# A third row buffer, other slots for VectorE's routing, transposes for a residual and two turnings, and a norm one slot later, in an encoder layer on one core

## The reference

```python
h = h + peer_ffn(rmsnorm(h, norm_ffn_g), peer_wq, peer_subkeys, peer_u, peer_v)

def peer_ffn(xn, w_q, sub_keys, u, v):
    q = (xf @ w_q).reshape(n, PEER_HEADS, 2, PEER_DK // 2)          # 8 heads, 2 x 128
    s = jnp.einsum('nhpd,hpkd->nhpk', q, sub_keys)                  # 128 keys a half
    sv, si = lax.top_k(s, PEER_TOPK)                                # 16 of them
    cand = sv[:, :, 0, :, None] + sv[:, :, 1, None, :]              # 256 pairs
    cidx = si[:, :, 0, :, None] * N_KEYS + si[:, :, 1, None, :]
    tv, tsel = lax.top_k(cand, PEER_TOPK)                           # 16 experts a head
    eidx = take_along_axis(cidx, tsel); g = softmax(tv)
    act = gelu(einsum('nd,ned->ne', x, u[eidx])) * g                # of 16384 experts
    return einsum('ne,ned->nd', act, v[eidx])
```

## Time and profile before

| | |
|---|---|
| median of 3 runs | 2055.32 us (2044.23, 2055.32, 2055.69) |
| profiled execution | 2047.77 us |
| its span | 2046.0 us |
| its mean granted clock | 0.988 |
| VectorE busy | 1530.7 us |
| ScalarE busy | 858.1 us |
| GpSimd busy | 718.3 us |
| HBM | 259 GB/s over the span |

### The profile page before, as it was taken

The page is one execution under the profiler, slowest core; times in us unless marked ns, Lnnn a source line. Parts: engine busy times, 40 slices in busy tenths (PEclk is TensorE's granted clock), DMA queues, the critical chain, the costliest instruction groups (busy, mean ns, idle before and its releaser), DMA issues. The chain is left out here.

```text
span 2046.0 us, 29568 instructions
## 1 busy us (share of the span) xinstructions
PE 1981.8 (97%) x11192; PEld 1765.1 (86%) x11192; DVE 1530.7 (75%) x2436; ACT 858.1 (42%) x857; POOL 718.3 (35%) x504
## 2 busy tenths in 40 slices
PE   7999998999899999999999999999999999999997
PEld 6987776998799999999999889988888888888886
DVE  5988745456678788989988987567677777778875
ACT  4340136334334554455454435433434343334343
POOL 2010110220726677587787875011001011114300
PEclk9999998999899999999999999999999999999999
DMA  5464393443344787788888787779998989998983
GB/s 207 164 193 141 116 400 137 153 168 123 127 137 156 247 275 268 272 281 286 274 272 298 265 306 283 294 274 348 340 343 328 343 326 349 364 360 345 372 314 136
DMA packets 101226, 531.27 MB, mean 260 GB/s; under 512 B 19376, under 2 KB 21568, under 8 KB 45792
## 3 DMA queue, kind: packets, MB, share of 16 engines
q1 hardware_dynamic: 71552, 408.93, 55.8%
q0 software_dynamic: 24304, 106.45, 14.4%
q10 hardware_dynamic: 5296, 14.98, 1.9%
HBM read 491.34 MB, written 38.14 MB: 259 GB/s over the span
## 5 line engine op out<-in xcount | busy, mean ns | idle before, releaser
L889 DVE TENSOR_TENSOR wl<-raw,wh 128x2048 fp32r<-128x2048 f32 x310 | 712.4, 2299 | 287.1 <-ACT wh L519 275.5
L519 ACT ACTIVATE wh<-raw 128x2048 fp32r<-128x2048 f32 x310 | 593.3, 1915 | 572.5 <-DMA raw<-in_v 408.4
L1537 PE MATMUL acc<-xhl,wh 128*128 128x448 f32 x2048 | 648.9, 377 | 12.2 <-DVE wl L889 12.2
L1538 PE MATMUL acc<-xhl,wl 128*128 128x224 f32 x2048 | 542.8, 265 | 0.0
L1537 PEld LDWEIGHTS acc<-xhl,wh 128*128 128x128 f32 x2048 | 386.7, 189 | 44.7 <-DVE wl L889 14.6
L1538 PEld LDWEIGHTS acc<-xhl,wl 128*128 128x128 f32 x2048 | 393.2, 192 | 0.0
L2025 POOL DMA_INDIRECT G<-gsum,cell x224 | 348.2, 1554 | 99.7 <-issue 74.8
L1514 PE MATMUL acc<-xhl,wh 128*128 128x288 f32 x768 | 231.7, 302 | 14.8 <-DVE wl L925 14.2
L1515 PE MATMUL acc<-xhl,wh 128*128 128x288 f32 x768 | 228.4, 297 | 0.0
L1516 PE MATMUL acc<-xhl,wl 128*128 128x288 f32 x768 | 227.9, 297 | 0.0
L1514 PEld LDWEIGHTS acc<-xhl,wh 128*128 128x128 f32 x768 | 146.5, 191 | 18.2 <-DVE wl L925 14.2
(11 more groups left out here) (306 smaller groups left out, 2638.8 us busy)
## 6 DMA issues: line engine op xcount, KB each, us to landing
raw<-in_u SPq DMA_DIRECT2D x128, 1024.0 KB
raw<-in_v SPq DMA_DIRECT2D x128, 1024.0 KB
raw<-in_w_mix SPq DMA_DIRECT2D x28, 1024.0 KB
G<-zero SPq DMA_DIRECT2D x16, 1024.0 KB, 13.8
raw<-in_w_out SPq DMA_DIRECT2D x16, 1024.0 KB
raw<-in_w_pq SPq DMA_DIRECT2D x16, 1024.0 KB
gin<-G SPq DMA_DIRECT2D x32, 512.0 KB
h<-hbg ACTq DMA_DIRECT2D x32, 448.0 KB
```

What stands on the lines that cost most here:

```text
L519: act.activation(wh[:, n % 4], raw[:, n % 4], ACT.Copy).then_inc(hi_done, 1)
L889: dve.tensor_tensor(wl[:, n % 4], raw[:, n % 4], wh[:, n % 4].bitcast(F32), ALU.subtract).then_inc(lo_done, 1)
L1537: pe.matmul(acc[:, s, 0:2 * NU], wh[:, s, j, :], xu[:, j, 0:2 * NU], start=(j == 0), stop=False)
L1538: ins = pe.matmul(acc[:, s, 0:NU], wl[:, s, j, :], xuh[:, j, :], start=False, stop=(j == DT - 1))
```

## The change

It has four parts. Routing: a third buffer `ring_a2` for own rows (the first 16 picks still use two, the other 16 use three in turn); new tables for the parts, tops, packs, sums, picks and own writes; for units of up to four heads one `wide_sum` of three operations over all 16 sums instead of 16 `gate_sum`; `own_hidden` waits for its own writes of the chunk before. Turnings: transposes instead of matmuls, behind slot 1 of iterations 29 and 30, with two banks copied out in a slot. Residual: 32 transposes ahead of V's first slot, which start the banks, the second token half first. PQ: `total(2)` behind slot 1, `scores(0, 0)` behind slot 2, and the splits for slot 3 ahead of the norm.

```diff
-XROW_IT, HST_IT = 29, 30
+XROW_IT, HST_IT, TURN_S = 29, 30, 1
+XROW_EVAC, HST_EVAC = 4 * XROW_IT + TURN_S + 1, 4 * HST_IT + TURN_S + 1
...
-PARTS = {4: (8, 1), 8: (9, 0), 12: (9, 1), 16: (4, 0), 20: (4, 1), 24: (5, 0), 28: (5, 1), 31: (10, 0), 35: (10, 1), 38: (11, 0),
-         42: (11, 1), 45: (6, 0), 49: (6, 1), 52: (7, 0), 56: (7, 1), 60: (12, 0), 64: (12, 1), 68: (13, 0), 73: (13, 1),
-         77: (14, 0), 81: (14, 1), 85: (15, 0), 90: (15, 1), 95: (16, 0), 99: (16, 1), 103: (17, 0), 107: (17, 1)}
-TOP = {12: 4, 28: 2, 42: 5, 56: 3, 73: 6, 90: 7, 107: 8}
+PARTS = {4: (8, 1), 5: (9, 0), 7: (9, 1), 12: (4, 0), 15: (4, 1), 17: (5, 0), 20: (5, 1), 29: (10, 0), 32: (10, 1), 35: (11, 0),
+         37: (11, 1), 44: (6, 0), 47: (6, 1), 49: (7, 0), 52: (7, 1), 63: (12, 0), 65: (12, 1), 68: (13, 0), 71: (13, 1),
+         79: (14, 0), 81: (14, 1), 84: (15, 0), 87: (15, 1), 101: (16, 0), 105: (16, 1), 109: (17, 0), 113: (17, 1)}
+TOP = {7: 4, 20: 2, 37: 5, 52: 3, 71: 6, 87: 7, 113: 8}
...
-SUMS = {1: 6, 2: 6, 3: 4, 5: 6, 6: 5, 7: 5, 15: 5, 17: 5, 19: 6, 31: 4, 32: 4, 33: 4, 36: 4, 37: 4, 39: 4, 40: 4, 41: 4,
-        46: 4, 47: 4, 48: 4, 51: 4, 53: 4, 54: 4, 55: 4, 57: 4, 59: 5, 61: 5, 62: 6, 63: 5, 65: 5, 66: 6,
-        76: 4, 78: 4, 79: 4, 80: 4, 82: 4, 84: 4, 86: 4, 88: 4, 93: 8, 94: 8, 96: 8, 98: 8}
+SUMS = {0: 16, 1: 16, 11: 16, 23: 8, 24: 4, 25: 8, 27: 8, 28: 4, 41: 16, 43: 16, 55: 4, 56: 8, 57: 4, 59: 8, 60: 4, 61: 4,
+        73: 8, 74: 4, 75: 8, 76: 4, 77: 8, 89: 4, 91: 8, 93: 4, 95: 8, 97: 4, 99: 4}
+WIDE_SUMS = 3
...
-           (0, 5): {4: 20}, (0, 6): {0: 21, 4: 22, 9: 23, 13: 24}, (0, 7): {0: 25, 3: 26, 8: 27, 13: 28}}
-A_CELLS = {(0, 1): 0, (1, 5): 1, (0, 3): 2, (1, 7): 3, (0, 5): 4}
...
+           (1, 7): {3: (15,), 15: (16,)}, (0, 4): {0: (17, 18)}, (0, 5): {0: (19,), 10: (20,)},
+           (0, 6): {0: (21,), 4: (22,), 9: (23,), 14: (24,)}, (0, 7): {0: (25,), 5: (26,), 11: (27,)}}
+A_CELLS = {(1, 4): 0, (0, 2): 1, (1, 6): 2, (0, 4): 3, (0, 6): 4, (0, 7): 5}
...
+def own_ring(g):
+    return g % 2 if g < K16 else (g - K16) % 3
...
 # ScalarE, pq (VectorE's the same with lo_next and norm_recip)
-                    hi_next(PQ0, i, s)
                     if first and s == 0:
+                        hi_next(PQ0, 0, 0)
+                        hi_next(PQ0, 0, 1)
                         norm_root(3, mis[:, 2], stat_done, 2)
+                    elif not (first and s == 1):
+                        hi_next(PQ0, i, s)
...
+            def wide_sum(m):
+                t, h = SUM_UNITS[m // K16]
+                u, width = HEADS * (1 - t), K16 * (h + 1)
+                eq = seq[:, 0:K16 * width].rearrange("p (r x) -> p r x", r=K16)
+                experts, gates = one(expert[:, t, 0:h + 1, :]), one(gij[:, 0, u:u + h + 1, :])
...
+                own.done(dve.tensor_tensor(eq, bcast(experts, K16, 1), bcast(expert[:, t, h, :], width, 2), ALU.is_equal))
+                own.wait(0)
+                own.done(dve.tensor_tensor(eq, eq, bcast(gates, K16, 1), ALU.mult))
+                own.wait(0)
+                dve.tensor_reduce(gsum[:, t, h, :], eq, AX.X, ALU.add).then_inc(sums_ready, K16)
...
             def act_lo(b, r):
+                if b == 1:
+                    dve.wait_ge(hst_out, 16)
...
 # TensorE, pq
-                    if first and s == 0:
+                    if first and s == 1:
                         pe.wait_ge(sq_done, 10)
                         total(2)
                         pe.wait_ge(sk_in, 16)
-                    if s > 0:
+                    if first and s == 2:
+                        scores(i, 0, first)
+                    if s > (1 if first else 0):
                         scores(i, s - 1, first)
...
-                    ins = pe.matmul(mis[:, c // 4, P * (c % 4):P * (c % 4) + P], xs4[:, c].rearrange("p q t -> p (q t)"), ident, start=True, stop=True)
+                    ins = pe.transpose(mis[:, c // 4, P * (c % 4):P * (c % 4) + P], xs4[:, c].rearrange("p q t -> p (q t)"), ident)
...
             def residual():
-                for d in range(DT):
-                    for t in range(2):
-                        ins = pe.matmul(banks[t][d // 4][:, P * (d % 4):P * (d % 4) + P], hT[:, d, P * t:P * t + P], ident, start=False, stop=False)
+                pe.wait_ge(hst_copied, 4)
+                for t in (1, 0):
+                    for d in range(DT):
+                        if t == 0 and d % 4 == 0:
+                            pe.wait_ge(acc_free, V0 + 1 + d // 4)
+                        ins = pe.matmul(banks[t][d // 4][:, P * (d % 4):P * (d % 4) + P], hT[:, d, P * t:P * t + P], ident,
+                                        start=(d % 4 == 0), stop=False, is_transpose=True)
                 ins.then_inc(res_turned, 1)
-            pe.wait_ge(hst_copied, 4)
-
-            def v_iteration(i, first=False, last=False):
+            residual()
+            def v_iteration(i, last=False):
...
                 if (t, h) in A_CELLS:
                     own_hidden(A_CELLS[t, h])
+            own_pick(28)
             own_pick(29)
-            own_hidden(5)
+            own_hidden(6)
```

## The result

The changed kernel takes 2039.22 us (median of 15 runs, 2033.26 to 2044.65) against 2052.30 (15 runs, 2044.23 to 2058.16): ratio 0.9935, 95% interval 0.9922 to 0.9947, 13 us faster. 2022 was forecast, and a saving of 29. The time lies inside the range given, by 0.8 us, only because that range was wide: 13 of the 29 us came, and the biggest term of the sum is the one that is missing. Its profiled execution took 2035.1 us with a span of 2033.3.

The account below looks back on a forecast made before the run. It took TensorE, busy 97% of the span, as the bound, plus its waits and lower-clock stretches. Savings of 5 + 13 + 6 + 5 = 29 us from a mean of 2050.8 gave 2022 us, range 2005 to 2040.

Parts of the forecast that it names:

- the rows: Product with `peer_u`: of 17.3 us lost to late splits and clock falls, 4 stay, 13 saved; pick 28 about 2 late.
- come as close: Product with `peer_u`, slots 38 and 42: picks 7 and 8 said to be as near to late as pick 28.
- Rival (1): Product with `peer_u`: rows stay late at picks 8 and 28, TensorE keeps 13 us of lateness; 2031 us, chance 0.15.
- VectorE's own work: Product with `peer_u`: with the new spread it stops TensorE nowhere; densest stretch 3 us late, under the 5 absorbed.
- The wide sums: VectorE's routing: 2.4, 3.2 and 4.0 us for units of 2, 3 and 4 heads; no change in its total.
- Three make 5.1: Product with `peer_u`: three clock falls behind waits for VectorE's split, 1.7 us each, counted in the 17.3 of lateness.
- Rival (2): The clock falls after each of three bursts of transposes, 1.7 us each; 2027 us, chance 0.08.
- The head of PQ: Start of the routing product: slot 1 ahead of `total(2)` cuts idle from 8.7 to 4.1 us; 5 saved, between 1 and 8.
- has over 5 us before slot 4: Head of PQ: ScalarE's split for slot 4 begins one slot later, with over 5 us to spare.
- Turnings: Tail of the product with `peer_u`: transposes take 1.92 us for 3.75, twice, and the idle and copy waits go; 6 saved.
- the step to V: Before the last product: 32 transposes take 3.8 us for 7.1 and hide a 1.9 wait; 5 saved, bounds 2 and 5.5.
- (5): Slower: at 2.45 us a descriptor in GpSimd's queue, TensorE stands still at slot 122; 42 lost, 2064 us, chance 0.03.

Follow-up runs that it names:

- early_picks: The changed kernel with picks 5 to 9 and 28 moved 3 to 20 writes earlier in GpSimd's queue; 2029.2 us, ratio 0.9882 to the kernel before.
- best: early_picks with ScalarE's split for PQ's slot 4 ahead of the first scores and picks 29 to 31 ahead of the last own writes; 2020.0 us, 0.9837.
- old_third: The changed kernel with the old routing tables and narrow sums, but three row buffers and picks from 21 on one place earlier; 2029.7 us, 0.9886.
- narrow: The changed kernel with the five wide sums done as 80 narrow ones in the same slots; 2036.2 us, ratio 0.9929 to the kernel before.

## Why the prediction was wrong

**The step that failed: the rows (13 us forecast, 0.3 measured).** The prediction put pick 28 in SBUF near slot 109.7 and its dot due near 109.3, a wait of 2 us with bounds at 8, and took 4 us of lateness. Its dot was due at slot 109.1, the row was there at 110.7, and VectorE waited 8.1 us. The end of unit (0,7) came at slot 107.9, close to the 107.5 forecast; what was left out are the four own writes of chunk 5, which the new `A_CELLS` puts behind that unit and so ahead of pick 28: 8.4 us. Half of the omission was hidden by luck, as the row could be read 5.6 us after its issue and not the 9.6 that the prediction took. It counted 24 own writes for the sum of the queue, but none for this place. Of the other picks, 7 and 8 were said to "come as close" and priced at nothing, and 5 and 6 weren't named; pick 7 was in time, while 5, 6 and 8 cost VectorE 2.9, 5.2 and 4.4 us, and TensorE 6.9 us ahead of slots 37 to 47. `early_picks` shows that this was all of it: with six picks moved, 3.9 us of waits and one fall of the clock (1.7 us) remained, where the prediction had taken 4 for both, and the stage was 12.5 us shorter. Rival (1), with 13 us of lateness kept and a chance of 0.15, was the mechanism, and named picks 8 and 28 for it. Its 2031 was still too low, since it kept 4 us of saving in this term and 5 in PQ.

**VectorE's own work.** That it would no longer stop TensorE was right (`best`: 3.9 us of waits). That this was needed was only half right: `old_third` gets the same time from the old spread. The wide sums cost 2.1, 2.9 and 3.7 us by the trace for 2.4, 3.2 and 4.0 forecast, and matter in nothing (`narrow`).

**The clock.** Before, three waits of 2.2 to 3.0 us had a fall behind them. After, one had (slot 37, 2.1 us), while waits of 3.0 and 2.6 us had none. "Three make 5.1" was a good account of one execution and not a price for a wait of a given length. Rival (2) was wrong: none of the four bursts of the kernel after had a fall behind it, and the falls in this stage, before and after, each stood right behind a wait of 2.1 us or more. Over the profiles of all 14 kernels here TensorE has 33 waits of 1.9 to 3.3 us in PQ and the product with `peer_u`; in 24 the clock fell before they ended or within 1.8 us behind them, in 9 it didn't.

**The head of PQ (5 forecast, 2.0 measured).** TensorE's wait was forecast as 4.1 us and was 4.2; GpSimd's sum was slowed by the second split as assumed. The step that failed is the sentence that slot 4's split "has over 5 us before slot 4": it was in time for slot 4 itself, but the copy of slot 3's queries stands behind it and the next split on VectorE. That gave 2.1 us of waiting and 1.7 of clock, against 4.5 us less of idle and 1.3 less lost to the clock behind `total(2)`: 2.0 in all. The queue behind the moved wait was followed one step too short.

**Turnings (6 forecast, 6.3 measured) and the step to V (5 forecast, 4.8 measured)** came out by their steps. The burst in the kernel after, timeline of TensorE:

```profile
1288.23 1.91 PE L1891 MATMUL mis<-cst,hT 128*32 128x128 f32 x16
```

1.9 us, without the 1.76 of idle ahead of it. The first residual's 0.6 us wait for `u_evac` lies where the prediction had put the evacuation.

**Base.** The sum was set against a mean of four executions, 2050.8; fifteen give a median of 2052.3. 1.5 us of the forecast's distance come from there. One sum in a rival is wrong too: in (5), 276 issues of 2.45 us are 676 us, 32 over the 644 and not 42, so that rival's time is 2054 and not 2064. Either lies within the 1% of no change, though the text books it as slower.

What stays open: why waits of the same length are followed by a fall of the clock once and not another time, and how far the new spread of VectorE's work helps with rows in time (1 us by the ratios of `old_third` and `early_picks`, 9 by the stage in two single profiles).

## What to carry to other kernels

When a buffer is added so that transfers can start earlier, follow each transfer's place in its issuer's queue: count every instruction between the last known point and the issue, and compare with when its reader is due, for each of them and not for one. A part that removes one wait in a chain of in-order queues is worth what the next wait leaves; the runs here went from pick 28 to pick 30 and from the sum to the query's copy. And a stage whose length wanders by several microseconds may have such a wait on its edge: with the picks moved, it was both shorter and steadier in three profiles of three.

## What the runs showed of the hardware

A long two-input operation of VectorE holds up GpSimd's indirect issues entirely, not by a share, and isn't held up by them. In the kernel after, 136 of GpSimd's indirect issues in the stage began while a split or a dot of VectorE ran; they took 2.22 us in the mean and ended 0.83 us behind the end of VectorE's instruction (half of them between 0.834 and 0.836). The 159 others took 1.0 us, also the 58 during which such an operation of VectorE began (0.97). VectorE's splits and dots took 2.29 us whether an issue was under way when they began or not. One such pair, GpSimd's the last write of (0,7), which ends 0.85 us behind the split that ran from 1207.29 to 1209.57:

```profile
1207.67 2.75 POOL L2077 DMA_INDIRECT G<-gsum,cell  x1 [0.30 <-issue]
```

```profile
1207.29 2.28 DVE L908 TENSOR_TENSOR wl<-raw,wh 128x2048 fp32r<-128x2048 f32 x1
```

With GpSimd's arithmetic it goes in both directions: at the head of PQ two splits took 3.1 and 4.1 us beside GpSimd's scaling of `xn`, where a split takes 2.29 else, and of the four scalings three took 2.4 us and one 4.45:

```profile
550.00 11.49 POOL L2024 TENSOR_TENSOR xn<-hT,rstd 128x1024 f32<-128x1024 f32 x4 [5.84 <-DVE rstd L934]
```

For the arithmetic this agrees with the Trainium skill (SBUF — State Buffer, SBUF: two separate sides), by which the shared pair of ports is an exclusive lock for the length of an instruction. It disagrees with that page on one point (Who interferes with whom): it infers that a two-input operation leaves the writing of descriptors alone, and the 136 issues here were held up by it.

So GpSimd's queue is coupled to VectorE's: a split or a dot makes an issue that begins in it about twice as long, and the mean price of an issue in the prediction, 1.55 us, is a mix of 1.0 and 2.2.
